# Half of the opening's transposes under the load, a split gated unit, one place of sums earlier, one block stored by accumulation

## The chip, the core and the metric

The kernel runs on one core of one Trainium2 chip. The engines are TensorE (PE in the profile, with PEld for its weight loads), VectorE (DVE), ScalarE (ACT), GpSimd (POOL) and SyncE (SP), and 16 DMA engines that all queues share. The metric is the time of the program on the device in microseconds (us), median of the runs shown.

## What is computed

A trunk of two layers over 512 tokens of 2048 channels, in float32. In each layer the input is scaled and shifted by a conditioning vector, goes through one input projection of 6144 columns, through four branches, and through one output projection, and is normalised:

```python
def reference(x, c, rel_bias, w_ada, b_ada, w_in, ...):
    cond = jax.nn.silu(c)
    for l in range(DEPTH):
        ada = cond @ w_ada[l] + b_ada[l]
        shift, scale, gate = jnp.split(ada, 3, axis=-1)
        h = x * (1.0 + scale[:, None]) + shift[:, None]
        proj = h @ w_in[l]
        ...
        y = gelu(y)                                        # S5 branch, 512 channels
        y_d = y * jax.nn.sigmoid(y @ w_glu + b_glu) * jax.nn.silu(d_g)
        y = jnp.concatenate([y_a, y_b, y_c, y_d], axis=-1) @ w_out[l]
        x = layer_norm(ALPHA * x + (1.0 + gate[:, None]) * y, ln_g[l], ln_b[l])
    return x
```

## The kernel before

**Products in three passes.** A float32 product of the projections is made of three fp32r passes: each operand is cut into a rounded part (`op_hi`, `w_hi`) and the rest (`op_lo`, `w_lo`), and hi x hi, hi x lo and lo x hi are added in a PSUM bank. The input projection runs in 4 steps (`ct`, 128 columns of each of 12 units) of 24 halves: a half `n` is one unit's 128 columns over 8 of the 16 channel tiles, 24 matmuls of 128x512. For a half, SP loads 512 KB into one of three `raw` slots (`raw_load`, L375), ACT writes `w_hi` (L671) and then minus raw into `w_lo` (L674), and a DMA issued by POOL adds raw to that (L604). The slot `raw[n % 3]` is free when PE has started the third pass of half `n`. In the output projection DVE makes `w_lo` by a subtraction instead.

**Sums of the conditioning.** The products `cond @ w_ada` that are not needed at the start are summed by DVE beside the steps, in 16 places of a step (`ada`). In layer 0 a place is two pieces `a` of 256 KB, in layer 1 one piece. They go through a ring of four tiles `ada_in`: SP waits before load `a` until DVE has used piece `a - 4` (`ada_load`, L446). `ADA_AT` says behind which half's `raw_load` the loads of a place stand on SP's queue, in each step after the first of layer 0; SP issues strictly in this order. On DVE, the first three places stand at the start of a step behind the preparation of the S5 weights, the fourth behind the convolution `xc`, and the others among the S5 scans. PE reads the scans' results in `s5_outputs` (L1077) after half 19.

**Opening.** While 32 tiles of `w_ada` of 1 MB each (`pro`) arrive, PE multiplies them (L915), turns the first 8 channel tiles of x (`channel`, L966), and runs the first half of four units (n = 0 to 3) between them. ACT makes `op_hi[k]` from the turned x in PSUM (`modulate`, L693) and, for even k, a second unrounded copy `hf` (L699); for odd k DVE makes it (L1567); DVE subtracts into `op_lo[k]` (L1562). When the last tile has come, `conditioning(1)` and `turn_sums(1)` give scale and shift of channels 8 to 15; only then are these turned, made, and multiplied, with half n = 4 (24 matmuls) running along; n = 5, 6, 7 follow.

**Gated unit.** `glu` (L1219) is 16 float32 matmuls of 128x512 straight from `w_glu` and `y_t`, between halves 5 and 6 of the output projection, once in each layer.

**End.** The last layer's result is normalised token block by token block (t = 0 to 3). For t = 0 and 1, `out` holds the row `ln_b` already; DVE makes (z - mean) x ln_g in two pieces, ACT scales them (L882), and a DMA of POOL adds them to `out` (L620). For t = 2 DVE does both operations on 2048 columns and SP stores it plainly, for t = 3 likewise in four pieces.

Of the kernel before, what the change touches and what calls it, by code (L numbers as in the profile page):

```python
# [67 lines left out]
DVE_LO = EARLY + 2  # L68
# [5 lines left out]
ADA_AT = (1, 2, 4, 5, 7, 8, 10, 11, 13, 14, 16, 17, 19, 22, 22, 23)  # L74
# [71 lines left out]
def trunk(nc, A, out):  # L146
# [5 lines left out]
    with ExitStack() as ctx:  # L152
# [12 lines left out]
        op_lo = [op[:, 2 * KT - 1 - k, :] for k in range(KT)]  # L165
        y_t = sb("y_t", [P, KT, S])
# [60 lines left out]
        gel = s5_s[3]  # L227
        gate_b = work[:, 0:4, :]
# [4 lines left out]
        scaled_pieces = [(t, D // 2 * i, D // 2 * (i + 1)) for t in range(2) for i in range(2)]  # L233
        whole_pieces = [(2, 0, D)] + [(3, S * i, S * (i + 1)) for i in range(4)]
# [8 lines left out]
        mix = work[:, 13, :]  # L243
        hf = work[:, 16:18, :]
# [39 lines left out]
        sums_turned = signal("sums_turned")  # L284

        class Layer:
            pass
        layers = []
        for l in range(DEPTH):
# [45 lines left out]
            s.glu_in = signal("glu_in" + n)  # L335
            s.glu_mm = signal("glu_mm" + n)
            s.glu_t = signal("glu_t" + n)
            s.gate_col = signal("gate_col" + n)
# [6 lines left out]
            s.d_done = signal("d_done" + n)  # L345
# [26 lines left out]
        def _(sp):  # L372
# [33 lines left out]
            for a in range(PRO_TILES):  # L406
# [5 lines left out]
                if a == 24:  # L412
                    x_load(1)
# [8 lines left out]
            for l, s in enumerate(layers):  # L422
# [36 lines left out]
                if l == 0:  # L459
                    raw_load(0, 0, DVE_LO - 1)  # L460
# [9 lines left out]
                for step in range(CT):  # L470
                    first = l == 0 and step == 0
                    for n in range(DVE_LO if first else 0, HALF):
# [22 lines left out]
                for n in range(W_OUT):  # L495
# [13 lines left out]
                    if n == 4:  # L509
                        sp.wait_ge(s.gate_col.sem, 1)  # L510
# [14 lines left out]
                    for i, name in ((0, "ln_g"), (1, "ln_b")):  # L525
                        if l and n == 11 + i:
                            sp.wait_ge(s.glu_mm.sem, 4)
                            sp.dma_start(ln_prev[:, i, :], A[name][l - 1].partition_broadcast(P))\
                                .then_inc(s.z_in.sem, 16)
                        if l == DEPTH - 1 and n == 10 + ST + i:  # L530
                            for to in (ln_last[i], *((out_v[:, 0, :], out_v[:, 1, :]) if i else ())):
                                sp.dma_start(to, A[name][l].partition_broadcast(P)).then_inc(s.ln_in.sem, 16)
# [16 lines left out]
        def _(pool):  # L549
# [67 lines left out]
            pool.wait_ge(layers[DEPTH - 1].ln_in.sem, 16 * 4)  # L617
# [6 lines left out]
        def _(act):  # L624
# [39 lines left out]
            for l, s in enumerate(layers):  # L664
# [19 lines left out]

                def channel_bank(k):
                    return bank[3 + k % 4 if l else EARLY_TURN[k // KH][k % KH % 3]][:, :]
# [15 lines left out]
                if l == 0:  # L702
# [4 lines left out]
                    for n in range(NHL, DVE_LO - 1):  # L707
                        split_hi_first(n)
                    for k in range(KH, KT):
                        modulate(k)  # L710
                    split_hi_first(DVE_LO - 1)
# [4 lines left out]
                def act_step(ct, first=False):  # L716
# [62 lines left out]
                    for n in range(DVE_LO if first else 2, HALF):  # L779
                        if first and n < DVE_LO + NHL:  # L780
# [1114 lines left out]
```

## Time and profile before

| | us |
|---|---|
| median of 3 runs | 1719.53 (1717.32 to 1721.11) |
| the profiled execution | 1719.88 |
| its span, first to last instruction | 1718.1 |
| PE busy in it | 1653.5 |
| opening, to the last `pro` tile | 115 |
| a step of layer 0 (ct 2) | 150.8 |
| a step of layer 1 | 148.2 |

The page of the profile gives each engine's busy time, the chain of work that ended last, and groups of instructions; the views named below show stretches of it. "Idle before" is the engine's wait ahead of an instruction, with what ended it.

### The profile page before, as it was taken

Reading aid. Unit: us, or ns where it says so; the run is one execution under the profiler, and the core shown is the slowest. Engines: PE = TensorE matmul, PEld = TensorE weight load, DVE = VectorE, ACT = ScalarE, POOL = GpSimd, SP = SyncE. Lnnn points to the kernel's source line nnn. Section 1 sums busy time; section 2 is a strip of 40 time slices with the busy share of each in tenths; the row PEclk is TensorE's granted clock in tenths of the full one; section 3 lists DMA queues with packets and bytes.
Section 4 is the critical chain, followed back from the end, with each engine's and each line's share of the span. In section 5 each row is a group of like instructions: output and inputs, shape, how many; then the busy total and the mean of one; then the engine's idle time right before and its main releaser. Section 6 shows DMA issues by size and latency. Waiting matters only on the chain.

```text
span 1718.1 us, 22890 instructions
## 1 busy us (share of the span) xinstructions
PE 1653.5 (96%) x7696; PEld 1269.4 (74%) x7696; DVE 1164.0 (68%) x2325; ACT 754.4 (44%) x988; POOL 179.4 (10%) x245
## 2 busy tenths in 40 slices
PE   5889999999999999999999999999999999999996
PEld 0347778778777877878887777777877777777885
DVE  1438975995697589657867685588378458743758
ACT  1316535554553555421127454654555465432112
POOL 2001111111111111000001111111111111100000
PEclk9799999999999999999999999999999999999998
DMA  9998899999999998978748888888988888775524
GB/s 364 339 317 212 204 245 245 219 220 221 242 226 231 238 220 204 215 248 274 246 145 203 196 206 195 205 199 208 209 203 208 192 200 204 188 184 218 196 94 116
DMA packets 317297, 373.58 MB, mean 217 GB/s; under 512 B 30584, under 2 KB 227536, under 8 KB 314512
## 3 DMA queue, kind: packets, MB, share of 16 engines
q1 hardware_dynamic: 288608, 270.57, 49.4%
q0 software_dynamic: 27936, 101.72, 33.1%
q8 instruction: 39, 0.64, 0.2%
q14 instruction: 58, 0.48, 0.1%
q10 hardware_dynamic: 656, 0.17, 0.0%
HBM read 263.89 MB, written 10.99 MB: 160 GB/s over the span
## 4 chain that ended last, share of the span: by engine, by line
PE 74%; DVE 17%; DMA 5%; issue 3%; ACT 1%; DVEq 0%; SPq 0%; ACTq 0%
PE bank L1232 19%; PE bank L1187 15%; PE bank L1197 15%; PE bank L1188 14%; DVE work L1562 6%; DMA pro<-in_w_ada 4%; PE bank L1219 2%; DVE work L1421 1%; DVE work L1422 1%; DVE y_t L1570 1%; PE bank L915 1%; DVE carry L1570 1%; DVE ada_acc L1570 1%; PE bank L1127 1%; PE bank L966 1%
## 5 line engine op out<-in xcount | busy, mean ns | idle before, releaser
L1187 PE MATMUL bank<-op,w_hi 128*128 128x512 f32 x1456 | 581.5, 399 | 0.2 <-ACT w_hi L671 0.2
L1188 PE MATMUL bank<-op,w_hi 128*128 128x512 f32 x1456 | 569.1, 391 | 0.0
L671 ACT ACTIVATE w_hi<-raw 128x1024 fp32r<-128x1024 f32 x188 | 199.2, 1059 | 418.9 <-PE bank L1188 286.5
L1197 PE MATMUL bank<-op,w_lo 128*128 128x512 f32 x1456 | 361.9, 391 | 3.6 <-DMA w_lo<-raw 3.6
L1187 PEld LDWEIGHTS bank<-op,w_hi 128*128 128x128 f32 x1456 | 274.1, 188 | 77.7 <-issue 21.6
L1197 PEld LDWEIGHTS bank<-op,w_lo 128*128 128x128 f32 x1456 | 273.7, 188 | 62.7 <-DMA w_lo<-raw 6.0
L1188 PEld LDWEIGHTS bank<-op,w_hi 128*128 128x128 f32 x1456 | 274.3, 188 | 56.6 <-issue 1.9
L604 POOL DMA_DIRECT2D w_lo<-raw x190 | 165.3, 870 | 1333.3 <-ACT w_lo L674 1124.3
L674 ACT ACTIVATE w_lo<-raw 128x1024 fp32r<-128x1024 f32 x188 | 198.4, 1055 | 98.1 <-PE bank L1197 96.6
L1232 PE MATMUL bank<-w_hi,op 128*128 128x512 f32 x960 | 232.2, 392 | 2.1 <-ACT op L861 2.1
L1232 PEld LDWEIGHTS bank<-w_hi,op 128*128 128x128 f32 x960 | 181.0, 189 | 41.0 <-issue 3.2
L1570 DVE SCALAR_TENSOR_TENSOR ada_acc<-ada_in,cond,ada_acc 128x512 f32<-128x512 f32 x225 | 169.1, 752 | 57.8 <-DMA ada_in<-in_w_ada 38.6
L845 ACT ACTIVATE w_hi<-raw 128x1024 fp32r<-128x1024 f32 x56 | 59.5, 1062 | 227.7 <-PE bank L1232 198.9
L1562 DVE TENSOR_TENSOR w_lo<-raw,w_hi 128x1024 fp32r<-128x1024 f32 x62 | 75.9, 1224 | 103.8 <-PE bank L1232 75.6
L1562 DVE TENSOR_TENSOR work<-bank,rot 128x512 f32<-128x512 f32 x128 | 88.5, 691 | 52.0 <-PE bank L1068 45.7
L1232 PE MATMUL bank<-w_lo,op 128*128 128x512 f32 x480 | 120.2, 389 | 0.0
L1232 PEld LDWEIGHTS bank<-w_lo,op 128*128 128x128 f32 x480 | 90.3, 188 | 18.8
L1562 DVE TENSOR_TENSOR work<-work 128x512 f32<-128x512 f32 x136 | 94.1, 692 | 4.6
L1562 DVE TENSOR_TENSOR work<-work,rot 128x512 f32<-128x512 f32 x112 | 77.5, 692 | 3.8
L915 PE MATMUL bank<-pro,work 128*32 128x512 f32 x256 | 48.0, 832 | 28.3 <-DMA pro<-in_w_ada 28.3
L915 PEld LDWEIGHTS bank<-pro,work 128*32 128x32 f32 x256 | 5.8, 125 | 58.6 <-DMA pro<-in_w_ada 52.4
L1422 DVE TENSOR_TENSOR_SCAN work<-s_k,carry,work 128x128 f32<-128x128 f32 x96 | 46.5, 484 | 3.4
(228 smaller groups left out, 1521.1 us busy)
## 6 DMA issues: line engine op xcount, KB each, us to landing
raw<-in_w_in SPq DMA_DIRECT2D x192, 512.0 KB, 4.6
w_lo<-raw POOLq DMA_DIRECT2D x190, 512.0 KB, 5.3
ada_in<-in_w_ada SPq DMA_DIRECT2D x256, 256.0 KB, 4.6
pro<-in_w_ada SPq DMA_DIRECT2D x32, 1024.0 KB, 10.1
raw<-in_w_out SPq DMA_DIRECT2D x64, 512.0 KB, 4.7
y_t<-in_x SPq DMA_DIRECT2D x2, 2048.0 KB, 12.9
bias_t<-bias_rows_scratch SPq DMA_DIRECT2D x16, 256.0 KB, 5.7
y_t<-in_x SPq DMA_DIRECT2D x4, 1024.0 KB, 8.1
```

The lines of the kernel that those rows point to most:

```text
L604: pool.dma_start(w_lo[:, n % NHL, :], raw[:, n % NRAW, :], accum_op=ALU.add)\
L671: act.activation(w_hi[:, n % NHL, :], raw[:, n % NRAW, :], ACT.Copy).then_inc(s.hi_done.sem, 1)
L674: act.activation(w_lo[:, n % NHL, :], raw[:, n % NRAW, :], ACT.Copy, scale=-1.0)\
L845: act.activation(out_hi[slot_of(n)], raw[:, n % NRAW, :], ACT.Copy).then_inc(s.hi_done.sem, 1)
L915: mm = pe.matmul(bank[2][32 * g:32 * g + 32, :], cond_rep[:, k, :], pro_ring[a % PRO_RING][:, S * g:S * (g + 1)], start=k == 0, stop=k == ...
L1187: pe.matmul(o, w_hi[:, n % NHL, w], op_hi[k], start=k == 0, stop=False)
L1188: mm = pe.matmul(o, w_hi[:, n % NHL, w], op_lo[k], start=False, stop=False)
L1197: mm = pe.matmul(o, w_lo[:, m % NHL, w], op_hi[k], start=False, stop=k == KT - 1)
L1232: mm = pe.matmul(bank[4 * (c % 2) + t][:, :], x[k][:, P * t:P * (t + 1)], w[slot_of(n)][:, S * j:S * (j + 1)], start=i == 0 and j == 0 and ...
L1422: own(dve.tensor_tensor_scan(b, mag, b, i_im, MUL, ADD), s.own)
L1562: return dve.tensor_tensor(o, a, b, op)
L1570: return dve.scalar_tensor_tensor(o, a, sc, b, op0, op1)
```

## The change

1. **Opening.** The channels 8 to 15 of x are turned during n = 2 and n = 3, at the places (n, j) of `TURNED_AT`, and ACT keeps each in `x_turned` in SBUF (`keep`). The load of x's second half is issued two tiles earlier. `modulate` and `modulated` read these copies. n = 4 and n = 5 run together (`two_units`), and DVE instead of ACT and POOL makes the lo part of n = 6.
2. **Gated unit.** w_glu and y are cut into hi and lo by ACT (two copies of 128x2048, behind `split_out(2)` and `split_out(3)`) and DVE (two subtractions, behind n = 3 and n = 4); PE runs 48 fp32r matmuls instead of 16 float32 ones.
3. **Sums.** In every step but the first, a fourth place of sums stands at the start of the step, and the one behind `s5_scan(2)` is gone. `ADA_AT` is new.
4. **End.** Block t = 2 is stored as t = 0 and 1 are, in two added pieces.

```diff
-DVE_LO = EARLY + 2
+DVE_LO = EARLY + 3
+TURNED_AT = {(2, 4): 8, (2, 6): 9, (3, 0): 10, (3, 2): 11, (3, 3): 12, (3, 4): 13, (3, 5): 14, (3, 6): 15}
...
-ADA_AT = (1, 2, 4, 5, 7, 8, 10, 11, 13, 14, 16, 17, 19, 22, 22, 23)
+ADA_AT = (0, 1, 2, 4, 5, 7, 8, 10, 11, 13, 16, 17, 19, 22, 22, 23)
...
-        scaled_pieces = [(t, D // 2 * i, D // 2 * (i + 1)) for t in range(2) for i in range(2)]
-        whole_pieces = [(2, 0, D)] + [(3, S * i, S * (i + 1)) for i in range(4)]
+        scaled_pieces = [(t, D // 2 * i, D // 2 * (i + 1)) for t in range(3) for i in range(2)]
+        whole_pieces = [(3, S * i, S * (i + 1)) for i in range(4)]
...
-                if a == 24:
+                if a == 22:
                     x_load(1)
...
+                def keep(k):
+
+                    act.wait_ge(s.h_bank.sem, k + 1)
+                    act.activation(x_turned[k], bank[EARLY_TURN[1][k % KH % 3]][:, :], ACT.Copy).then_inc(x_kept.sem, 1)
...
+                    if n == 2:
+                        act.wait_ge(s.step_end.sem, s.step_end.at(0, CT))
+                        act.wait_ge(s.op_lo.sem, KT + 4)
+                        act.activation(glu_y_hi, y_t[:, 12:16, :], ACT.Copy).then_inc(s.glu_hi.sem, 1)
+                    if n == 3:
+                        act.wait_ge(s.glu_in.sem, s.glu_in.at(16))
+                        act.wait_ge(s.op_lo.sem, KT + 8)
+                        act.activation(glu_w_hi, w_glu, ACT.Copy).then_inc(s.glu_hi.sem, 1)
...
+                        if (n, j) in TURNED_AT:
+                            channel(TURNED_AT[n, j])
...
+                def two_units():
+
+                    a, b = EARLY, EARLY + 1
+                    o_a, o_b = (bank[EARLY_BANK[u]][:, :] for u in range(2))
+                    pe.wait_ge(s.hi_done.sem, s.hi_done.at(b + 1))
+                    for j in range(KH):
+                        k, w = KH + j, slice(P * j, P * (j + 1))
+                        pe.wait_ge(s.op_hi.sem, k + 1)
+                        pe.matmul(o_a, w_hi[:, a % NHL, w], op_hi[k], start=False, stop=False)
+                        pe.matmul(o_b, w_hi[:, b % NHL, w], op_hi[k], start=False, stop=False)
+                        if j == 0:
+                            pe.wait_ge(first_lo_done.sem, a + 1)
+                        mm = pe.matmul(o_a, w_lo[:, a % NHL, w], op_hi[k], start=False, stop=False)
...
+                        pe.wait_ge(s.op_lo.sem, k + 1)
+                        mm_a = pe.matmul(o_a, w_hi[:, a % NHL, w], op_lo[k], start=False, stop=k == KT - 1)
+                        mm_b = pe.matmul(o_b, w_hi[:, b % NHL, w], op_lo[k], start=False, stop=False)
+                    mm_a.then_inc(s.mm_done.sem, 1)
+                    mm_b.then_inc(s.hi_used.sem, 2)
...
-                            mm = pe.matmul(bank[4 + m][:, :], w_glu[:, k, P * m:P * (m + 1)], y_t[:, 12 + k, :],
-                                           start=k == 0, stop=k == 3)
+                            w = slice(P * m, P * (m + 1))
+                            pe.matmul(bank[4 + m][:, :], glu_w_hi[:, k, w], glu_y_hi[:, k, :], start=k == 0, stop=False)
+                            pe.matmul(bank[4 + m][:, :], glu_w_hi[:, k, w], glu_y_lo[:, k, :], start=False, stop=False)
+                            mm = pe.matmul(bank[4 + m][:, :], glu_w_lo[:, k, w], glu_y_hi[:, k, :], start=False, stop=k == 3)
...
                 ada(2, 1)
+                if not first:
+                    ada(2, 1)
...
                 s5_scan(2)
-                ada(2, 1)
+                if first:
+                    ada(2, 1)
...
-                    for n in range(NHL + 2, DVE_LO - 1):
-                        first_lo(n)
+                    first_lo(EARLY)
                     conditioning(1)
                     for k in range(KH, KT):
                         modulated(k)
-                    first_lo(DVE_LO - 1)
+                        if k == KH + 2:
+                            first_lo(EARLY + 1)
                     all_modulated()
+                    first_lo(EARLY + 2)
...
+                    if n == 3:
+                        dve.wait_ge(s.glu_hi.sem, s.glu_hi.at(1))
+                        tt(glu_y_lo, y_t[:, 12:16, :], glu_y_hi.bitcast(F32), SUB).then_inc(s.glu_lo.sem, 1)
+                    if n == 4:
+                        dve.wait_ge(s.glu_hi.sem, s.glu_hi.at(2))
+                        dve.wait_ge(s.op_lo.sem, KT + 12)
+                        tt(glu_w_lo, w_glu, glu_w_hi.bitcast(F32), SUB).then_inc(s.glu_lo.sem, 1)
```

On SP, from the last half of step 1 of layer 0 into step 2 (the first row is the load of half 23, the row behind it place 15; the loads of `raw` from there on are halves 0, 1, 2, ... of step 2, those of `ada_in` its places 0, 1, 2, ...). Before:

```order
L382 DMA raw<-in_w_in 128x8x128 [waits raw_used_0]
L449 DMA ada_in<-in_w_ada 128x512 [waits ada_used_0] x2
L382 DMA raw<-in_w_in 128x8x128 [waits raw_used_0] x2
L449 DMA ada_in<-in_w_ada 128x512 [waits ada_used_0] x2
L382 DMA raw<-in_w_in 128x8x128 [waits raw_used_0]
L449 DMA ada_in<-in_w_ada 128x512 [waits ada_used_0] x2
L382 DMA raw<-in_w_in 128x8x128 [waits raw_used_0] x2
L449 DMA ada_in<-in_w_ada 128x512 [waits ada_used_0] x2
```

The same stretch of SP after the change:

```order
L399 DMA raw<-in_w_in 128x8x128 [waits raw_used_0]
L466 DMA ada_in<-in_w_ada 128x512 [waits ada_used_0] x2
L399 DMA raw<-in_w_in 128x8x128 [waits raw_used_0]
L466 DMA ada_in<-in_w_ada 128x512 [waits ada_used_0] x2
L399 DMA raw<-in_w_in 128x8x128 [waits raw_used_0]
L466 DMA ada_in<-in_w_ada 128x512 [waits ada_used_0] x2
L399 DMA raw<-in_w_in 128x8x128 [waits raw_used_0]
L466 DMA ada_in<-in_w_ada 128x512 [waits ada_used_0] x2
L399 DMA raw<-in_w_in 128x8x128 [waits raw_used_0] x2
L466 DMA ada_in<-in_w_ada 128x512 [waits ada_used_0] x2
```

Place 2 (pieces 4 and 5) stood behind the loads of halves 3 and 4 and now stands ahead of both, behind the load of half 2.

On PE, the end of n = 3 and the start of the second half of the opening after the change:

```order
L1056 MATMUL bank1<-op,w_lo 128x512 x3
L1071 MATMUL bank5<-op,w_hi 128x512 [waits op_hi_done_0,hi_done_0]
L1072 MATMUL bank6<-op,w_hi 128x512
L1075 MATMUL bank5<-op,w_lo 128x512 [waits first_lo_done]
L1079 MATMUL bank5<-op,w_hi 128x512 [waits op_lo_done_0]
L1080 MATMUL bank6<-op,w_hi 128x512
```

Where a transpose and three matmuls stood for each channel, five matmuls for two units (banks 5 and 6) stand now, and no transpose.

## Rows read from the trace of the kernel before

**Rows 1.** The page: busy time, share of the span and instructions of engines.

```profile
PE 1653.5 (96%) x7696; PEld 1269.4 (74%) x7696; DVE 1164.0 (68%) x2325; ACT 754.4 (44%) x988; POOL 179.4 (10%) x245
```

**Rows 2.** Timeline, opening: start, duration, engine, line, operation, tiles [idle before <-releaser].

```profile
93.25 0.43 DVE L1567 TENSOR_SCALAR rot<-rot 128x512 f32<-128x512 f32 x1
...
114.57 1.06 PE L915 MATMUL bank<-pro,work 128*32 128x512 f32 x8 [0.47 <-DMA pro<-in_w_ada]
...
119.23 0.17 DVE L1570 SCALAR_TENSOR_TENSOR hs<-bank,ada_b 128x8 f32<-128x8 f32 x1
...
121.70 0.81 DVE L1567 TENSOR_SCALAR work<-bank,hs 128x512 f32<-128x512 f32 x1
...
145.35 1.42 DVE L1562 TENSOR_TENSOR work<-bank,rot 128x512 f32<-128x512 f32 x2 [0.46 <-PE bank L1068]
```

**Rows 3.** One line's instructions, 120 to 132 us: loads of raw, issue and landing.

```profile
L382 SPq DMA_DIRECT2D raw<-in_w_in x2: 433/507/581, 124.0 to 124.5; - x2
...
DMA to landing us min/median/max: 6.6/7.1/7.6
```

**Rows 4.** Chain of work that ended last (start, us, what), gated unit of layer 0.

```profile
746.10 13.73 PE bank L1219 x32
```

**Rows 5.** Timeline of ACT, output projection of layer 0 ahead of it.

```profile
736.71 1.06 ACT L845 ACTIVATE w_hi<-raw 128x1024 fp32r<-128x1024 f32 x1 [7.59 <-DMA raw<-in_w_out]
```

**Rows 6.** Chain: third passes (8 matmuls) of half 3, in steps 1 and 2.

```profile
280.31 1.82 PE bank L1197 x8
...
431.04 1.82 PE bank L1197 x8
```

**Rows 7.** Timeline of SP, start of step 2: raw 3 and 4, place 2, raw 5.

```profile
414.97 5.82 SPq L382 DMA_DIRECT2D raw<-in_w_in  x2
...
424.50 1.48 SPq L449 DMA_DIRECT2D ada_in<-in_w_ada  x2
...
426.02 0.93 SPq L382 DMA_DIRECT2D raw<-in_w_in  x1
```

**Rows 8.** Timeline of DVE and PE, the same stretch.

```profile
417.16 0.17 DVE L1351 COPY s_k<-s5c 128x16 f32 x1 [4.38 <-issue]
...
423.96 0.51 DVE L1566 TENSOR_SCALAR ada_acc<-ada_in,cond 128x512 f32<-128x512 f32 x1
...
427.25 0.39 PE L1187 MATMUL bank<-op,w_hi 128*128 128x512 f32 x1
```

**Rows 9.** Timeline, step 1: DVE's first sums, as 423.96 in step 2.

```profile
268.84 0.49 DVE L1566 TENSOR_SCALAR ada_acc<-ada_in,cond 128x512 f32<-128x512 f32 x1
```

**Rows 10.** Issue to landing: raw, four loads from 407 to 426; page, medians.

```profile
DMA to landing us min/median/max: 3.9/4.7/6.4
...
raw<-in_w_in SPq DMA_DIRECT2D x192, 512.0 KB, 4.6
w_lo<-raw POOLq DMA_DIRECT2D x190, 512.0 KB, 5.3
```

**Rows 11.** Waits in steps 1 to 3, and timeline of DVE and SP, step 2.

```profile
PE bank L1077 <- DVE work L1562: 1.5, 1, 1.5
...
496.16 1.54 DVE L1570 SCALAR_TENSOR_TENSOR ada_acc<-ada_in,cond,ada_acc 128x512 f32<-128x512 f32 x2
...
493.89 1.05 SPq L449 DMA_DIRECT2D ada_in<-in_w_ada  x2
```

**Rows 12.** Busy time by 2 us (PE, PEld, DVE, ACT, POOL, clock, DMA share, GB/s).

```profile
174.00:176.00 2.00, 2.00 (x6) 1.51 (x6) 1.79 (x7) 0.00 (x0) 0.00 (x0) 0.50 1.11 290
```

**Rows 13.** Timeline, the end, DVE; and landing of the four additions into out.

```profile
1697.06 1.28 DVE L1570 SCALAR_TENSOR_TENSOR y_t<-y_t,mv,work 128x1024 f32<-128x1024 f32 x1
...
1702.12 2.35 DVE L1570 SCALAR_TENSOR_TENSOR y_t<-y_t,mv,work 128x2048 f32<-128x2048 f32 x1
...
1714.78 0.75 DVE L1570 SCALAR_TENSOR_TENSOR y_t<-y_t,mv,ada_in 128x512 f32<-128x512 f32 x1
...
DMA to landing us min/median/max: 5.4/8.4/9.1
```

More of the change, by code:

```diff
@@ L243, in trunk @@
         mix = work[:, 13, :]
+        x_turned = {KH + i: work[:, at, :] for i, at in enumerate((5, 6, 10, 11, 12, 13, 14, 15))}
         hf = work[:, 16:18, :]
@@ L284, in trunk @@
         sums_turned = signal("sums_turned")
+        x_kept = signal("x_kept")
         class Layer:
@@ L288, in trunk, with both_layers @@
         layers = []
+        in_both = {}
+        def both_layers(name, each):
+            if name not in in_both:
+                in_both[name] = signal(name)
+            return Signal(in_both[name].sem, 0, each * len(layers))
         for l in range(DEPTH):
@@ L471, in _ @@
                     first = l == 0 and step == 0
-                    for n in range(DVE_LO if first else 0, HALF):
+                    for n in range(DVE_LO - 1 if first else 0, HALF):
                         if step or n >= NRAW:
@@ L530, in _ @@
                         if l == DEPTH - 1 and n == 10 + ST + i:
[L531 removed]
+                            for to in (ln_last[i], *((out_v[:, t, :] for t in range(3)) if i else ())):
                                 sp.dma_start(to, A[name][l].partition_broadcast(P)).then_inc(s.ln_in.sem, 16)
@@ L777, in after @@
                         return unit_end(UNITS.index(name), first) + 2
-                    for n in range(DVE_LO if first else 2, HALF):
-                        if first and n < DVE_LO + NHL:
-                            act.wait_ge(first_lo_done.sem, n + 1 - NHL)
-                        split_hi(n, ct)
+                    for n in range(DVE_LO - 1 if first else 2, HALF):
+                        if first and n < DVE_LO:
+                            split_hi_first(n)
+                        else:
+                            if first and n < DVE_LO + NHL:
+                                act.wait_ge(first_lo_done.sem, n + 1 - NHL)
+                            split_hi(n, ct)
                         if n == after("d_u"):
@@ L956, in channel @@
                         last = k - 3 if i >= 3 else KH * half - 1
-                        if last >= 0:
+                        if half and i >= 3:
+                            pe.wait_ge(x_kept.sem, i - 2)
+                        elif last >= 0:
                             pe.wait_ge(s.op_hi.sem, last + 1)
@@ L962, in channel @@
                                 pe.wait_ge(s.hf_done.sem, last // 2 + 1)
-                        if i == 2:
-                            pe.wait_ge(s.hs.sem, half + 1)
+                        if half == 0 and i == 2:
+                            pe.wait_ge(s.hs.sem, 1)
                     for t in range(ST):
@@ L971, in early_pass @@
                     u, half = half_unit(n, True)
-                    o, fresh = bank[EARLY_BANK[u]][:, :], u == 0
+                    o, fresh = bank[EARLY_BANK[u]][:, :], n == 0
                     if fresh:
-                        ahead = [k for k in range(2) if EARLY_TURN[half][k] != 2]
+                        ahead = [k for k in range(2) if EARLY_TURN[0][k] != 2]
                         for k in ahead:
-                            channel(KH * half + k)
-                        turn_sums(half)
+                            channel(k)
+                        turn_sums(0)
                         for k in range(len(ahead), 2):
-                            channel(KH * half + k)
+                            channel(k)
                     pe.wait_ge(s.hi_done.sem, s.hi_done.at(n + 1))
@@ L1008, in early_pass, with early_lo @@
                         lo_ready(n, 0)
+                    early_lo(n, o)
+                def early_lo(n, o):
+                    half = half_unit(n, True)[1]
                     for j in range(KH):
```

69 lines of the change are left out of this document (45 added, 24 removed).

## Prediction

> **What bounds the kernel now.** I read the page first: PE is busy for 1653.5 of 1718.1 us [rows 1], so the time is PE's, and an edit counts only where it takes work from PE or moves a wait of PE. That leaves 65 us in which PE stands: most of them in the opening, the rest in small waits and at the end. Then I read the stretches that the change touches: the timeline of the opening (when does the first product that DVE and the S5 branch wait for come?), the chain of work around the gated unit, the timelines of SP, DVE and PE at the start of a step, the waits of steps 1 to 3, and the timeline of the end. The working is made against the profiled execution, 1719.88 us (span 1718.1, so 1.8 us lie around it). It stands 0.35 above the median of 1719.53, so the same sum on the median is 0.35 lower.
>
> **1. Opening.** The last `pro` tile is multiplied at 114.57, and PE had waited for it by DMA: nothing before this moves the end [rows 2]. `hs` is ready at 119.40. From there to the first S5 input (DVE at 145.35) is one chain: 8 channels turned, each a transpose, an ACT pass and DVE passes from PSUM (0.81 each), 24 matmuls of n = 4, then n = 5, the convolution's copy and its product [rows 2]. Behind it DVE, not PE, sets the pace of step 0 for a long time, so what matters is when 145.35 comes. After the change the x's are in SBUF: the DVE operation on such an operand takes 0.43 [rows 2] and no transpose stands between. DVE then needs, for the 8 channels, 8 subtractions of 0.69, 4 copies of 0.43 and one 1024-wide subtraction of 1.22, 8.5 us. They can begin at `hs`, since no channel has to be turned first: 119.4 and 8.5 give 127.9, and PE's five last matmuls (1.1) end the two units at 129. The next limit is half 6: its raw load is issued at 124.0 and lands after 6.6 us, at 130.6 [rows 3]; one ACT pass of 1.06 (as in [rows 5]) gives 131.7. From there I count 4.3 us for the products of half 6 that stand ahead of the convolution, and 4.7 for the convolution's copy and product and its S5 input (5.7 from copy to DVE before), so DVE's S5 input comes at about 140.7 instead of 145.35: **-4.7**. If half 6's load were no limit it would be -6.5; if PE, waking from its wait at half clock, and ACT's copies under the load cost all that can be read of such things (2 to 3 us), -2. PE's eight transposes in n = 2 and 3 (about 0.5 us each) lie in waits for `pro` tiles, DMA-bound as above; if they were not covered, they would cost 4.
>
> The same copies have a price: the ACT pass then reads SBUF. The Trainium skill ("VectorE: DVE Perf Modes", section "The TRN2 errata — SBUF-src ops pay a fixed extra latency per instruction") gives ScalarE 224 cycles of fixed cost from SBUF against 172 from PSUM, which works out as an estimate of some 0.04 us an operation, or 0.3 us over 8; no row of mine is needed for it and it changes neither sum nor chances, but for DVE the row goes the other way than that heading says (0.43 from SBUF against 0.81 from PSUM, [rows 2]), and the row decides.
>
> **2. Gated unit.** 16 float32 matmuls take 13.73 us [rows 4], once a layer. A pass of fp32r of the same shape goes at 1.82 for 8, 0.227 each [rows 6]; 48 of them are 10.9. Saved: 2.85 in each layer, **-5.7** in both (-5.4 to -6.0, by a granted clock that may differ a little). The two copies (ACT, about 2 us each for 2048 elements, from 1.06 for 1024 in [rows 5]) and two subtractions (DVE, 2.35 each [rows 13]) lie beside the halves 2 to 5: ACT stands idle 7.59 us for a load at 736.71, just in this stretch [rows 5], and the unit starts at 746.10. If that cover were gone, they would show once as a wait of up to 2 us.
>
> **3. Sums: SP's queue.** This edit looks like it moves only DVE's work, but `ADA_AT` moves the loads. In steps 1 to 3 of layer 0, place 2 (pieces 4 and 5) now stands on SP ahead of the raw loads of halves 3 and 4. A load of piece 4 waits until DVE has used piece 0 in the ring of four; SP waits there, and the raw loads queue behind. When does DVE use piece 0 and 1? In step 2 it starts its first sums at 423.96, behind the preparation of the S5 weights [rows 8], and SP's loads of place 2, waiting for them, span 424.50 to 425.98; only the next raw load (half 5) at 426.02 is behind them [rows 7]. Now half 3 takes that place. Before, its load was issued at 414.97 [rows 7], so it comes 11 us later. From there:
> - landing 5.0 (3.9 on quiet engines, 6.4 behind others, median 4.7 [rows 10]): 431.0;
> - ACT's w_hi 1.06, so PE's first pass can start at 432.2, where it started at 427.25 [rows 8]: 4.9 us of standing;
> - ACT's second pass and POOL's start, 1.4, and the addition's landing 5.3 [rows 10]: w_lo is whole at 438.7. The third pass started at 431.04 [rows 6]: **+7.7**.
>
> Halves 4 and 5 come behind in the same order and have their slots already, so the delay is not made larger, and PE has no slack further on to take it back: the S5 inputs, the attention and DVE's scans all start from PE's products. Step 3 shows the same rows as step 2, a step later: **+7.8**. In step 1 DVE is earlier: its sums start at 268.84 [rows 9], 155.1 ahead of step 2's where a step is 150.7, so raw(3) goes out at about 270.8 instead of 264.3 (414.97 less a step); half 3's third pass can start at 283.6 instead of 280.31 [rows 6]: +3.3. A standing PE also loses its clock: at 174 to 176, behind a stretch in which PE mostly stood, the granted clock is 0.50 [rows 12], that is 1.2 GHz; that costs about 1.7 us in step 1, while in steps 2 and 3 it runs off within the wait for w_lo. Step 1: **+5.0**. Sum **+20.5**. Ends: with every landing at the quiet end (3.9, and no clock) 14.6; with 6.4 and a second loss of clock, 32. In layer 1 a place is one piece, four places fit the ring, and nothing is blocked: 0.
>
> The Trainium skill ("DMA: Bandwidth & Descriptors", section "Latency and other measured facts") says that a lighter load on HBM makes the fixed cost of a transfer smaller. The loads of a step's start come one at a time in the new order; by that rule they would land like the quietest row, 3.9 [rows 10], and the three stalls would each be 1.1 us shorter, 3.3 in all. That is inside the ends above.
>
> **4. Sums: DVE's chain.** In each of steps 1 to 3 PE waits 1.5 us at the S5 outputs for DVE [rows 11], and behind `s5_scan(2)` one place of 1.54 us is gone: that would be -4.5 in all. But the places slide by one: what DVE uses at 496.16 is now place 10, not 9 [rows 11], and place 10's loads stand behind raw(16) as before, issued about 493.89 [rows 11]. Taken at 4.3 (a little under the 4.7 of the larger raw load [rows 10]), they land at 498.2 or later. DVE waits for them, with the scans that PE waits for behind it. Net of the 1.54 removed I get +1.9, +0.5 and +0.4 for the three steps, **+2.8** (ends -4.5, if the loads are early, and +5, if they land like loads in a crowd).
>
> **5. End.** From 1702 on DVE works without a gap to the last 512-wide piece, which starts at 1714.78 [rows 13]; it is DVE that ends the kernel, with one store behind it. Block t = 2 is two operations of 2.35 [rows 13] before. After: one half of 1.28 [rows 13], 0.18 for the reciprocal, and one of 1.2, as for t = 0 and 1; ACT and POOL take the rest. That shortens DVE's chain by 2.3. What can come late instead is POOL's added pieces: they land after 5.4 to 9.1 us [rows 13], at one per 2.4 us where four are in flight. Issued near 1705 and 1706.3, t = 2's would land at 1712.7 and 1715.2, ahead of DVE's own last store. So **-2.2**, with -0.3 if they land last.
>
> **Sum.** -4.7 - 5.7 + 20.5 + 2.8 - 2.2 = +10.7; 1719.88 + 10.7 = 1730.6, and on the median **1730**.
>
> **Rivals.**
> - *A smaller stall.* DVE stands 4.38 us at 417.16, at the step's start, released by nothing that the profile shows [rows 8]; step 3 has the like, step 1 has not, and there the sums come 4.4 us earlier by [rows 9]. Should it go away in the changed program (it has other code around it), the sums start 4.4 earlier and the stalls of steps 2 and 3 shrink by 4.4 each: 20.5 becomes 11.7, the time 1730.2 - 8.8 = **1721.4**, no change. For it: step 1. Against: the same code in the same order stands ahead of it.
> - *The faster side: DVE is early for both.* The same early sums, and place 10's data in time at 496: then part 4 is -4.5, not +2.8, and the time is 1721.4 - 7.3 = **1714**. If SP did not stand at place 2 at all, it would be 1702.5: -12.6 for parts 1, 2 and 5 and -4.5. It decides at the time of DVE's first sums: from about 414 on (10 us earlier than now) SP is free. Against: SP's row shows the wait for exactly this signal, at 424.50.
> - *A larger stall.* Raw(3) lands like 6.4 and w_lo behind the pieces that are now loaded beside it; two losses of clock. Then 28 to 32 instead of 20.5: **1738 to 1742**.
> - *The opening gives nothing.* The early load of x and the transposes delay the last `pro` tile by what they save behind it: +4.7, **1735**.
>
> **Chances.** Forecast 0.55; smaller stall 0.10; faster side 0.17; larger stall 0.12; opening gives nothing 0.06. A measurement of this kernel tells apart about 0.2%, 3.4 us: faster is below 1716.1, slower above 1723.0. Faster 0.17, same 0.10, slower 0.73. The range 1712 to 1740 leaves out the far part of the faster side and of the larger stall, less than 2 in 10.
>
> **What would show it.** In steps 1 to 3 of layer 0: SP's load of half 3 directly behind place 2, 11 us later than before in steps 2 and 3; PE idle ahead of the first pass of half 3 by about 5 us (released by ACT's w_hi) and ahead of its third by 1 to 3 (released by the DMA into w_lo), in step 1 only the latter; the granted clock low in those slices. Steps 2 and 3 near 160 us instead of 150.8. DVE waiting for `ada_in` behind the third S5 input. The gated unit at 10.9 us. DVE's first S5 input at about 140.7. Two pieces of 1024 for t = 2. Wrong would be: no idle PE at half 3, which makes it a faster kernel at once; a last `pro` tile later than 114.6; or the end set by POOL's additions.

## The result

| | kernel before | changed kernel |
|---|---|---|
| median of the runs | 1718.72 us (4 runs) | 1758.87 us (1757.32 to 1761.4, 4 runs) |
| ratio to before | | 1.0232 (95% interval 1.0219 to 1.0246) |
| span of the profiled execution | 1718.1 | 1758.3 |

The change makes the kernel 40 us slower. The forecast was slower by 10.7 us, 1730 in all, with a range from 1712 to 1740: the sign and the first cause were right, the size was a quarter of the real one. What it priced wrongly is part 4: the late loads of place 10 were to cost 2.8 us net in layer 0 and nothing in layer 1, and one number that puts them right is worth 29 us.

The first place to look is the fifth part of the page, the costliest groups of instructions, each with the time that its engine stood idle just ahead and who ended it. The rows are PE's first pass (w_hi, first of its pair) and third pass (w_lo) of all halves of the steps. Of the kernel before:

```profile
L1187 PE MATMUL bank<-op,w_hi 128*128 128x512 f32 x1456 | 581.5, 399 | 0.2 <-ACT w_hi L671 0.2
...
L1197 PE MATMUL bank<-op,w_lo 128*128 128x512 f32 x1456 | 361.9, 391 | 3.6 <-DMA w_lo<-raw 3.6
```

Of the changed kernel:

```profile
L1260 PE MATMUL bank<-op,w_hi 128*128 128x512 f32 x1456 | 584.4, 401 | 11.7 <-ACT w_hi L688 11.6
...
L1270 PE MATMUL bank<-op,w_lo 128*128 128x512 f32 x1456 | 367.8, 396 | 28.8 <-DMA w_lo<-raw 28.8
```

The work is the same; PE stands 36.7 us more ahead of it, 11.5 for w_hi and 25.2 for w_lo. To see where, I took from both timelines the start of the third pass of every half, and noted wherever the distance between the two kernels grew or shrank:

| stretch | measured | forecast |
|---|---|---|
| opening and step 0 of layer 0 | -3.1 | -4.7 |
| half 3 of steps 1, 2, 3 of layer 0 | +5.6, +8.8, +8.4 = +22.8 | +20.5 |
| halves 16 and 17 of the same steps | +5.4, +3.2, +1.4 = +10.0 | with the next row |
| S5 outputs of the same steps | -1.5, -1.6, -0.9 = -4.0 | +2.8 |
| gated unit of layer 0 and the turn of layers | -1.8 | -2.85 |
| halves 16 and 17 of steps 0 to 3 of layer 1 | +4.9, +5.1, +5.1, +1.3 = +16.4 | 0 |
| gated unit of layer 1 | -2.8 | -2.85 |
| from PE's end to the end of the program | +2.1 | -2.2 |
| changes under 0.3 us each, together | +0.6 | |
| sum | +40.2 | +10.7 |

**Half 3, the forecast cause.** SP in step 2 (the timeline: start, duration, queue, line, operation), which answers to [rows 7]. The first row is place 2, waiting for DVE's first sums, and the raw loads of halves 3 and 4 come behind it; half 3's went out at 414.97 in the kernel before, and the changed kernel is 6.6 us behind at that point, so it is 10.6 late:

```profile
431.04 1.11 SPq L466 DMA_DIRECT2D ada_in<-in_w_ada  x2
432.20 1.06 SPq L399 DMA_DIRECT2D raw<-in_w_in  x2
```

The same stretch on ACT, which waits for the load, and on PE, which waits for ACT and then for the addition into w_lo:

```profile
438.00 1.06 ACT L688 ACTIVATE w_hi<-raw 128x1024 fp32r<-128x1024 f32 x1 [13.77 <-DMA raw<-in_w_in]
...
439.11 0.79 PE L1260 MATMUL bank<-op,w_hi 128*128 128x512 f32 x1 [5.10 <-ACT w_hi L688]
...
446.32 1.89 PE L1270 MATMUL bank<-op,w_lo 128*128 128x512 f32 x7 [1.45 <-DMA w_lo<-raw]
```

The forecast was a wait of 4.9 ahead of the first pass; it is 5.10. The second wait is only 1.45 because PE's own pass took longer: its matmul takes 0.79 at 439.11, and the windows (length, busy times of PE, PEld, DVE, ACT, POOL; then granted clock, DMA share, GB/s) give half clock, 0.50, around the end of the wait and behind it:

```profile
438.00:440.00 2.00, 0.89 (x2) 0.80 (x3) 0.00 (x0) 2.00 (x3) 0.00 (x0) 0.50 1.07 339
440.00:442.00 2.00, 2.00 (x6) 1.51 (x6) 1.50 (x2) 1.95 (x5) 0.86 (x1) 0.50 1.12 337
```

**Halves 16 and 17, the cause that was missed.** Step 0 of layer 1, where nothing was forecast. DVE around the tenth place (the row behind it is `score_max(3)`), ACT's softmax (L765), the next w_hi behind it in ACT's queue, which is half 16's, its addition on POOL, and half 16's third pass on PE:

```profile
1032.00 0.75 DVE L1648 SCALAR_TENSOR_TENSOR ada_acc<-ada_in,cond,ada_acc 128x512 f32<-128x512 f32 x1 [3.37 <-DMA ada_in<-in_w_ada]
1032.68 0.68 DVE L1528 CUSTOM_DVE_ANT_0 work<-bank,bias_t 128x512 f32<-128x512 f32 x1
...
1034.57 0.40 ACT L765 ACTIVATE work<-work,soft 128x128 f32<-128x128 f32 x1 [4.90 <-DVE soft L1644]
...
1037.73 1.05 ACT L688 ACTIVATE w_hi<-raw 128x1024 fp32r<-128x1024 f32 x1
...
1040.02 0.86 POOL L621 DMA_DIRECT2D w_lo<-raw  x1 [9.19 <-ACT w_lo L691]
...
1047.63 3.48 PE L1270 MATMUL bank<-op,w_lo 128*128 128x512 f32 x8 [3.25 <-DMA w_lo<-raw]
```

The kernel before in the same place:

```profile
1004.41 0.75 DVE L1570 SCALAR_TENSOR_TENSOR ada_acc<-ada_in,cond,ada_acc 128x512 f32<-128x512 f32 x1
...
1007.23 0.40 ACT L738 ACTIVATE work<-work,soft 128x128 f32<-128x128 f32 x1 [1.91 <-DVE soft L1566]
...
1012.67 0.86 POOL L604 DMA_DIRECT2D w_lo<-raw  x1 [6.20 <-ACT w_lo L674]
...
1019.87 1.98 PE L1197 MATMUL bank<-op,w_lo 128*128 128x512 f32 x8
```

Read it as a chain. The load of place 10 stands behind raw(16), at 1027.4; DVE wants it at about 1028.6, since its place is now where place 9's was; it lands 4.4 us after its issue. DVE waits 3.37, the row maximum is late by as much, ACT waits 4.90 where it waited 1.91, and w_lo of half 16, which stands in ACT's queue behind the softmax, is 3.0 late against the kernel's shift at that point (1040.02 less 1012.67 is 27.35, the shift 24.35). Its addition lands after 7.6 us (5.1 before), and PE waits 3.25. Then its eight matmuls take 3.48 for 1.98, at half clock:

```profile
1048.00:1050.00 2.00, 2.00 (x6) 1.52 (x6) 1.76 (x3) 0.00 (x0) 0.00 (x0) 0.50 0.57 124
```

That is 4.9 us of one late load of 256 KB: 3.0 by which ACT is late and 2.5 by which the addition lands later, less 2.1 of slack (before, it landed 2.1 ahead of the third pass), and 1.5 for the slower matmuls.

The last step of each layer loses only 1.3 to 1.4, and the same sum gives it. In step 3 of layer 1, DVE and ACT are as late as above:

```profile
1491.63 0.75 DVE L1648 SCALAR_TENSOR_TENSOR ada_acc<-ada_in,cond,ada_acc 128x512 f32<-128x512 f32 x1 [3.37 <-DMA ada_in<-in_w_ada]
...
1505.11 2.12 PE L1270 MATMUL bank<-op,w_lo 128*128 128x512 f32 x8 [1.11 <-DMA w_lo<-raw]
```

But the addition lands after 5.4 us, not 7.6, and the granted clock behind the wait of 1.11 stays at 1.00: 3.0 and 0.4, less 2.1 of slack, is 1.3. What differs beside it in the other steps is two loads of `bias_t`, the next step's bias, which SP issues at 1039.61 and 1040.25, within half a us of the addition at 1040.02; in the last step there are none. That these loads are the reason is argued from the rows; no run moves them alone.

**The end.** DVE's last operation ends 9.2 us behind PE's last matmul instead of 11.5, as forecast. But the program ends 6.9 us behind DVE, where it was 2.6. The plain stores (one line's DMAs, issue to landing, min/median/max) take, before and then after; the 5.6 before is the large store of t = 2, the four of t = 3 took 2.1 each:

```profile
DMA to landing us min/median/max: 2.1/2.1/5.6
```

```profile
DMA to landing us min/median/max: 4.3/4.9/6.1
```

They share the DMA engines with the two pieces of t = 2 that POOL adds, which land after 7.4 and 9.3 us. Still, they are not what ends the program: the last store lands at 1755.8, 2.5 us ahead of the end (0.4 ahead before). What ends last is the DRAIN that stands behind POOL's last DMA, an instruction that isn't counted as busy and stands in no chain of the page (one line's instructions: duration in ns, first and last start), in the changed kernel and then in the kernel before:

```profile
L153 POOLq DRAIN  x1: 13665/13665/13665, 1744.4 to 1744.4; - x1
```

```profile
L152 POOLq DRAIN  x1: 13280/13280/13280, 1701.2 to 1701.2; - x1
```

It ends at 1758.03, 0.2 us ahead of the program's end, where before it ended 3.6 ahead. In all profiles of this case it ends 4.25 to 4.34 us behind the landing of POOL's last addition.

### The profile page after: what moved, and what is told of

It reads as the page before. It is cut to its first block, busy times and chain, and to the rows that moved or that the text cites. A ratio compares the mean times of both kernels' runs of the same rounds, so it can differ in the third digit from the quotient of the medians.

```text
span 1758.3 us, 22981 instructions
## 1 busy us (share of the span) xinstructions
PE 1660.3 (94%) x7728; PEld 1281.3 (73%) x7728; DVE 1169.5 (67%) x2330; ACT 767.4 (44%) x1001; POOL 181.2 (10%) x246
## 4 chain that ended last, share of the span: by engine, by line
PE 77%; DMA 11%; DVE 6%; ACT 2%; issue 2%; SPq 0%; DVEq 0%; ACTq 0%
PE bank L1307 18%; PE bank L1270 16%; PE bank L1260 15%; PE bank L1261 15%; DMA w_lo<-raw 4%; DMA pro<-in_w_ada 3%; DMA ada_in<-in_w_ada 2%; DVE work L1640 2%; PE bank L953 1%; PE bank L1197 1%; PE bank L1185 1%; DVE y_t L1648 1%; DMA raw<-in_w_in 1%; PE bank L1004 1%; PE bank L1138 1%
## 5 line engine op out<-in xcount | busy, mean ns | idle before, releaser
L1270 PE MATMUL bank<-op,w_lo 128*128 128x512 f32 x1456 | 367.8, 396 | 28.8 <-DMA w_lo<-raw 28.8
L1499 DVE TENSOR_TENSOR_SCAN work<-s_k,carry,work 128x128 f32<-128x128 f32 x96 | 46.5, 484 | 3.4
L1498 DVE TENSOR_TENSOR_SCAN work<-s_k,carry,work 128x128 f32<-128x128 f32 x96 | 46.5, 484 | 3.4
```

The lines of the kernel that those rows point to most:

```text
L1270: mm = pe.matmul(o, w_lo[:, m % NHL, w], op_hi[k], start=False, stop=k == KT - 1)
L1498: own(dve.tensor_tensor_scan(a, mag, a, i_re, MUL, ADD), s.own)
```

## The experiments

Each time is beside runs of the kernel before on the same chip; ratios are to those.

**Place 10's loads at half 14.** One number of the changed kernel:

```diff
-ADA_AT = (0, 1, 2, 4, 5, 7, 8, 10, 11, 13, 16, 17, 19, 22, 22, 23)
+ADA_AT = (0, 1, 2, 4, 5, 7, 8, 10, 11, 13, 14, 17, 19, 22, 22, 23)
```

> The changed kernel with one number of ADA_AT altered: the loads of place 10 stand behind the raw load of half 14, not 16 (where the changed kernel uses them one place earlier on DVE than before). Theory (place 10 is loaded too late for its new position; DVE waits some 3.4 us for it, the softmax on ACT behind it is late, and with it ACT's w_hi of half 16): the stalls at halves 16 and 17 go, 10 us in layer 0 and 16.4 in layer 1, so some 26 us less than the changed kernel, about 1732. Rival (those stalls come from something else in the change, such as the fourth place at the step's start pushing DVE back, or the load on the DMA engines): less than 3 us gained, 1756 or more.

Measured: 1731.51, ratio 1.0064 (1.0046 to 1.0081). The page's row of PE's third passes in this kernel:

```profile
L1270 PE MATMUL bank<-op,w_lo 128*128 128x512 f32 x1456 | 361.1, 390 | 9.1 <-DMA w_lo<-raw 9.1
```

From 28.8 to 9.1 us idle, and no growth at halves 16 and 17 of any step behind step 0; half 3 grows by 5.4, 8.2 and 8.3 as before. The rival is out: this one number is worth 0.0168 in the ratio, 29 us.

**Place 2's loads at half 4.**

```diff
-ADA_AT = (0, 1, 2, 4, 5, 7, 8, 10, 11, 13, 16, 17, 19, 22, 22, 23)
+ADA_AT = (0, 1, 4, 4, 5, 7, 8, 10, 11, 13, 16, 17, 19, 22, 22, 23)
```

> The changed kernel with one other number of ADA_AT altered: the loads of place 2 stand behind the raw load of half 4, as before the change, not behind half 2. Theory (SP waits at place 2 for DVE and the raw loads of halves 3 and 4 queue behind it): the stalls at half 3 in steps 1 to 3 of layer 0 go, 22.9 us, about 1736; layer 1 unchanged. Rival (DVE, now with four places at the start of a step, holds the step up by itself): the stall stays or moves to the convolution, a gain under 10 us, 1749 or more.

Measured: 1736.72, ratio 1.0108 (1.0073 to 1.0143). PE's idle ahead of the first passes is gone; of what is left ahead of the third passes, 18.3 us stand at half 16 of the seven steps:

```profile
L1260 PE MATMUL bank<-op,w_hi 128*128 128x512 f32 x1456 | 581.8, 400 | 0.1
...
L1270 PE MATMUL bank<-op,w_lo 128*128 128x512 f32 x1456 | 366.8, 395 | 22.4 <-DMA w_lo<-raw 22.4
```

**Both numbers.**

```diff
-ADA_AT = (0, 1, 2, 4, 5, 7, 8, 10, 11, 13, 16, 17, 19, 22, 22, 23)
+ADA_AT = (0, 1, 4, 4, 5, 7, 8, 10, 11, 13, 14, 17, 19, 22, 22, 23)
```

> The changed kernel with both numbers altered (place 2 behind half 4, place 10 behind half 14). Theory, both causes being separate: the gains add up to 49 us, about 1709.5, which is faster than the kernel before by the opening, the gated unit and the 1.5 us waits at the S5 outputs. Rival (the two stalls share slack: where one is taken away, the other grows): 1715 to 1725.

Measured: 1710.23, ratio 0.9936 (0.9919 to 0.9952), and in a second series on another chip 1708.58, 0.9935. The two causes add up: by the ratios 29 and 21 us singly, 51 together. What the change brings is seen undisturbed here: the third passes stand 4.8 us earlier at the end of step 0 (2.3 to 5.5 in the other kernels with this opening, 0.5 in the one below that moves the row maximum), gain 1.5 or 1.6 more at the S5 outputs of each of steps 1 to 3, and 3.3 at the turn of layers.

**Sums undone.** `ADA_AT` and DVE's places as before, all else changed:

```diff
-ADA_AT = (0, 1, 2, 4, 5, 7, 8, 10, 11, 13, 16, 17, 19, 22, 22, 23)
+ADA_AT = (1, 2, 4, 5, 7, 8, 10, 11, 13, 14, 16, 17, 19, 22, 22, 23)
...
-                if not first:
-                    ada(2, 1)
...
-                if first:
-                    ada(2, 1)
+                ada(2, 1)
```

> The changed kernel with its third part undone wholly: ADA_AT and the places of sums on DVE as in the kernel before; the opening, the gated unit and the end stay changed. Theory: opening -3, gated unit -5.7, end +2 against the kernel before, about 1712, and the 1.5 us waits at the S5 outputs of steps 1 to 3 are there again. Rival (the opening's or the end's change also feeds the later stalls): above 1720.

Measured: 1713.0, ratio 0.995 (0.9931 to 0.997). PE's wait for DVE at the S5 outputs is there again (us in total, times, longest):

```profile
PE bank L1147 <- DVE work L1637: 4.8, 3, 1.6
```

The third part of the change is thus the whole loss. With its loads put right it is a gain by the trace, three times the 1.5 us of [rows 11], but the ratios, 0.995 and 0.9936, differ by 2.4 us and their intervals overlap.

**Who is the victim.** The changed kernel with the late load left as it is, but with the row maximum ahead of the tenth place:

```diff
-                ada(2, 1)
-                score_max(3)
+                score_max(3)
+                ada(2, 1)
```

> The changed kernel, with both numbers as the change has them; on DVE the tenth place of sums stands behind score_max(3) instead of ahead of it. Its loads are as late as in the changed kernel, so DVE waits as long; what changes is who waits for DVE. Theory (the stall of PE at halves 16 and 17 comes over ACT's softmax, which needs score_max(3), and ACT's w_hi and w_lo of half 16 behind it in its queue): PE's stalls at halves 16 and 17 in steps 1 to 3 of both layers are gone or under 1 us each, and DVE's wait reaches PE at the S5 outputs instead, 0 to 3 us a step; 1733 to 1745 in all. Rival (DMA load or the raw loads themselves are late): the stalls stay, 1755 or more.

Measured: 1732.09, ratio 1.0068 (1.0048 to 1.0089), 0.9 under the stated range. No growth at halves 16 and 17 of steps 1 to 3 of layer 0 or of any step of layer 1. ACT's wait ahead of the softmax in step 0 of layer 1, in this kernel:

```profile
1025.80 0.40 ACT L765 ACTIVATE work<-work,soft 128x128 f32<-128x128 f32 x1 [1.91 <-DVE soft L1644]
```

It is 1.91 again, exactly as before the change. So the stall runs over the row maximum, the softmax and ACT's queue, and not over the load on the DMA engines or the raw loads. The wait of DVE shrank too, as its place is later (0.66 us in that step instead of 3.37), so the expectation that DVE waits as long did not hold, and a part of the gain may be this. In step 0 of layer 0, 5.3 us are lost at halves 22 and 23; two other kernels with this opening lose 2.2 and 2.4 there, so that only the rest can be the order's.

**The mismatch alone.** The kernel before, with one number altered, which puts the loads of place 9 two halves later:

```diff
-ADA_AT = (1, 2, 4, 5, 7, 8, 10, 11, 13, 14, 16, 17, 19, 22, 22, 23)
+ADA_AT = (1, 2, 4, 5, 7, 8, 10, 11, 13, 16, 16, 17, 19, 22, 22, 23)
```

> The kernel before the change, with one number of ADA_AT altered: place 9's loads stand behind the raw load of half 16, not 14. It makes the same mismatch between load and use as the change does for place 10, and nothing else of the change. Theory: DVE waits for these loads, and PE at halves 16 and 17 in steps 1 to 3 of layer 0 and all steps of layer 1: 20 to 28 us more than before, 1739 to 1747. Rival (the mismatch costs only together with the fourth place at the start of the step, or with the opening): under 5 us more, below 1724.

Measured: 1750.36, ratio 1.0175 (1.0154 to 1.0195), a little over the range: 30 us. Growth at halves 16 and 17: 5.0, 5.0 and 1.2 in layer 0 (with 1.5 given back at the S5 outputs of the first two), 5.0, 7.6, 5.5 and 1.4 in layer 1. No part of the change is needed for the stall but the distance between load and use.

**The queue alone.** The kernel before, with place 2 ahead of raw loads 3 and 4:

```diff
-ADA_AT = (1, 2, 4, 5, 7, 8, 10, 11, 13, 14, 16, 17, 19, 22, 22, 23)
+ADA_AT = (1, 2, 2, 5, 7, 8, 10, 11, 13, 14, 16, 17, 19, 22, 22, 23)
```

> The kernel before the change, with one number of ADA_AT altered: place 2's loads stand behind the raw load of half 2, not 4, so ahead of raw loads 3 and 4. Nothing else of the change. Theory (SP waits there for DVE's first sums): PE stands at half 3 in steps 1 to 3 of layer 0 as in the changed kernel, some 23 us, layer 1 as before; 1738 to 1743. Rival (the stall needs the fourth place at the step's start): under 5 us, below 1724.

Measured: 1740.82, ratio 1.0118 (1.0097 to 1.014): 20 us, the forecast's own number for this cause, without the fourth place at the step's start. In the trace, steps 2 and 3 lose 7.8 and 7.2 at half 3, and step 1 loses 3.8 there and 1.8 soon behind it.

**The gated unit.** The kernel of both numbers, with PE's products as before; the four cut operands are made and not read:

```diff
-                            pe.matmul(bank[4 + m][:, :], glu_w_hi[:, k, w], glu_y_hi[:, k, :], start=k == 0, stop=False)
-                            pe.matmul(bank[4 + m][:, :], glu_w_hi[:, k, w], glu_y_lo[:, k, :], start=False, stop=False)
-                            mm = pe.matmul(bank[4 + m][:, :], glu_w_lo[:, k, w], glu_y_hi[:, k, :], start=False, stop=k == 3)
+                            mm = pe.matmul(bank[4 + m][:, :], w_glu[:, k, w], y_t[:, 12 + k, :], start=k == 0, stop=k == 3)
```

> The kernel of both altered numbers, with the gated unit's products as 16 float32 matmuls from w_glu and y_t again; ACT and DVE still make the four cut operands, which nothing reads. Theory (the unit is on PE's path at both layers, 10.9 against 13.7 us): 5.7 us more than with both numbers alone, about 1716. Rival (PE's gain is given back behind it, where the weights of the output projection are waited for): no difference, 1710.

Measured: 1715.15, ratio 0.9975 (0.996 to 0.9989), that is 0.39% or 6.7 us more than with both numbers alone, where 5.7 was worked out; the intervals of the two leave 1.4 to 12, so the rival is out and the size is read from the trace. In the changed kernel's chain of work the unit stands between these two runs of output products (start, us, what): the first ends at 774.03, the second starts at 784.91, 10.88 us for 13.73 in [rows 4].

```profile
739.29 34.74 PE bank L1307 x144
...
784.91 15.19 PE bank L1307 x67
```

**The end.** Block t = 2 plain again, on the kernel of both numbers:

```diff
-        scaled_pieces = [(t, D // 2 * i, D // 2 * (i + 1)) for t in range(3) for i in range(2)]
-        whole_pieces = [(3, S * i, S * (i + 1)) for i in range(4)]
+        scaled_pieces = [(t, D // 2 * i, D // 2 * (i + 1)) for t in range(2) for i in range(2)]
+        whole_pieces = [(2, 0, D)] + [(3, S * i, S * (i + 1)) for i in range(4)]
```

A first kernel with this edit kept DVE's test on t and so left out the second DVE operation on block t = 2 (the product with 1 / deviation and the sum with `ln_b`); its time is that of less work, and nothing is built on it.

> The kernel of both altered numbers, with block t = 2 stored plainly by SP again, as before the change (no added pieces, two DVE operations of 2048). Theory (the added pieces of t = 2 take longer to land than DVE saves, and hold up the last plain stores on the same DMA engines: 6.9 us from DVE's last operation to the end where it was 2.6): 2.0 us less than with both numbers alone, about 1708, with 2.6 us behind DVE's last operation. Rival (the longer end is a chance of the profiled execution): 2.3 us more than with both numbers alone, about 1712.5.

Measured: 1705.35, ratio 0.9914 (0.9897 to 0.9931). With all operations, beside a second series of the kernel of both numbers on the same chip:

> The kernel of both altered numbers, with block t = 2 made wholly by DVE (two operations of 2048) and stored plainly by SP, as before the change. Theory (the added pieces of t = 2 land later than DVE saves, and the last plain stores wait behind them on the same DMA engines): 2.0 us less than with both numbers alone on the same chip, and 2.6 us between DVE's last operation and the end. Rival (the longer end is a chance of the profiled executions): 2.3 us more.

> The kernel of both altered numbers once more, on the same chip as the one with the plain end, so that two us can be told apart. Both theories: 0.5 to 0.65% under the kernel before, about 1709 to 1711; with 4 to 7 us between DVE's last operation and the end by the theory of the end, 2.6 by the rival.

Measured: 1707.55, 0.9929 (0.9912 to 0.9946), against 1708.58, 0.9935 (0.9916 to 0.9954). The times alone don't tell 2 us apart: the difference is 1.0 and the intervals overlap almost wholly. The profiles do. From PE's last matmul to the end of the span there are 14.0 us in each of the four profiles with a plain and whole t = 2 (14.02 to 14.03) and 15.8 to 16.4 in each of the eight with added pieces. The last operation of DVE, plain (span 1706.6) and added (span 1704.9):

```profile
1703.32 0.75 DVE L1648 SCALAR_TENSOR_TENSOR y_t<-y_t,mv,ada_in 128x512 f32<-128x512 f32 x1
```

```profile
1697.26 0.75 DVE L1648 SCALAR_TENSOR_TENSOR y_t<-y_t,mv,ada_in 128x512 f32<-128x512 f32 x1
```

2.5 us stand behind the first, 6.9 behind the second. So the added end costs about 2.1 us (1.8 to 2.4) where it was to save 2.2. In each of the eight profiles with it, POOL's last addition lands 4.56 us ahead of the end and POOL's DRAIN ends 0.2 ahead, the last of all engines' work; in the four with a plain and whole t = 2 the DRAIN ends 3.0 to 4.8 ahead and the last store decides. The kernel with both numbers put right and the plain end is the best that was run, 0.7% under the kernel before, though not told from the one with the added end by its time.

## Why the forecast was right and wrong

- **SP's queue, right mechanism, a little too small.** Place 2 ahead of raw(3) stops SP until DVE's first sums, and PE stands at half 3 in steps 1 to 3 and not in layer 1. Worked out 20.5; measured 22.8 in the trace, 21 by taking it away and 20 by putting it alone into the kernel before. The term too small is the landing: 5.0 us was taken for raw(3); it took 6.6, 5.7 and 5.4 in steps 1, 2 and 3, with 6.0 for the addition (5.3 taken). So PE waits 1.9 ahead of the first pass in step 1 too, where only the third was to wait. Here the sentence on a rule of the Trainium skill ("DMA: Bandwidth & Descriptors", section "Latency and other measured facts": lighter HBM load, smaller fixed cost) was used on a false premise. Once SP is free it issues two raw loads and four pieces within 5 us, so the engines are busier, not quieter: the window at 438 moves 339 GB/s. The rule isn't contradicted, the load was.
- **Place 10, right place and wrong price: the step that failed.** Part 4 has +2.8 for it in layer 0 and nothing in layer 1; measured are +10.0 less 4.0 in layer 0 and +16.4 in layer 1, and 29 us by taking the late load away. "Place 10's loads stand behind raw(16) as before ... DVE waits for them": that wait is there. Two things failed. First, its reach: it was counted for steps 1 to 3 of layer 0 alone, since layer 1 had been settled with the sentence "nothing is blocked: 0", which was true of the ring and of SP and says nothing of this. The places slide by one in every step that isn't the first of the program, and layer 1 has four of them: 16.4 us. Second, the victim: I followed what stands behind the wait on DVE as far as the scans and the S5 outputs, "with the scans that PE waits for behind it", and not the very next operation, `score_max(3)`. It releases ACT's softmax, and ACT's queue holds w_hi and w_lo of half 16. So 10.0 in layer 0 where the wait was to cost a part of what the removed place saved. The saving itself is right: 1.5 and 1.6 at the S5 outputs of steps 1 and 2 (0.9 in step 3).
- **The clock, undersized.** PE runs at 0.50 of its clock for some us behind the wait at half 3 in each of the three steps, and behind the waits of 3.0 to 3.7 us at half 16 in steps 0 and 1 of layer 0 and 0 to 2 of layer 1, where a wait of 3.25 becomes 4.9. Behind the waits of 2.98, 1.27 and 1.11 at the other halves 16 it stays at 1.00. The forecast took 1.7 us for it in one place.
- **Opening, right to the first S5 input.** 140.7 was forecast for it; it came at 141.01. It didn't keep: the distance is -6.0 at half 11, -2.5 at half 17 and -3.1 at the step's end. In step 0 DVE leads, as the forecast said, and half 16 then waits on the same road as above, over DVE's softmax values and ACT, here without a late load: in the kernel of both numbers, ACT's softmax starts at 190.76, 6.6 earlier than before, but PE is 8 us ahead by then and waits 3.5 for w_lo of half 16. The second profile of the same kernel has no growth there and loses 2.2 at halves 22 and 23 instead, for a reason that was not followed. The step of part 1 that failed is taking the gain at the S5 input for the gain at the step's end. The row of the changed kernel that answers to the last of [rows 2]:

```profile
141.01 1.41 DVE L1640 TENSOR_TENSOR work<-bank,rot 128x512 f32<-128x512 f32 x2
```

- **Gated unit, right.** 10.88 us for 10.9. About 1 us of it is missing at the turn of layers in the changed kernel; with both numbers right the whole 3.3 shows there. Where that 1 us goes was not followed.
- **End, wrong sign.** DVE's chain is 2.3 us shorter, as said. What failed in part 5 is the bound: the term took the landing of POOL's pieces, compared it with DVE's last store and allowed -0.3 "if they land last". The program doesn't end at that landing but 4.56 us behind it, with POOL's DRAIN. This is the sign that the prediction itself named, "the end set by POOL's additions". It also left out that the plain stores behind them share the engines: 4.3 to 6.1 us instead of 2.1. That alone would have used up the gain: with 0.4 us behind the last store, as before, the end would come 14.0 behind PE's last matmul, as before (an estimate from the rows above); the DRAIN puts 2.1 on top. The bound should have gone above nothing.
- **Rivals.** None of them came. The 4.4 us of idle at the step's start, on which the rival of a smaller stall rested, is there again: the first sums of step 2 start at 430.52, which is 423.96 and the shift of 6.6. The larger stall went in the right direction with the wrong reason: half 3 lost 22.8, not 28 to 32.

## What to carry to other kernels

A table that says when loads are issued has two sides, and a change in the order of use must be checked against both: whether an early load blocks the queue for what stands behind it, and whether a late one now comes after its use, in every loop and every layer that reads the table. And where an engine waits in order, price the wait by the first operation behind it that another engine needs, not by the one where the old wait was seen; then follow that other engine's queue as well.

## What the runs showed of the hardware

- A late load of 256 KB, 3.4 us for DVE, cost 4.9 us of PE, over two engines' queues, a DMA that landed in 7.6 us where it took 5.1, and a granted clock of 0.50 for some 3 us behind the wait.
- Not every wait cost clock: of the eight waits at half 16, the granted clock was 0.50 for some 3 us around or behind five (3.03 to 3.66 us) and stayed at 1.00 behind three (1.11, 1.27 and 2.98).
- Plain stores of 256 KB behind two accumulating DMAs of 512 KB landed in 4.3 to 6.1 us, and in 2.1 without them.
- The DRAIN behind POOL's last DMA ended 4.25 to 4.34 us after that DMA had landed, in all thirteen profiles. With an added block t = 2 it ended last of all, and the program was 2.1 us longer though DVE was done 2.3 us earlier.
